# A two-block transformer kernel: the opening sums eight modulation tiles on TensorE and takes the norm statistics per token

## What is computed

```python
cond = jax.nn.silu(c)                                   # c: (1, 1024)
mod = cond @ w_ada[layer] + b_ada[layer]                # (1, 3072)
shift, scale, gate = jnp.split(mod, 3, axis=-1)
h = rmsnorm(x, g_pre[layer]) * (1.0 + scale[:, None, :]) + shift[:, None, :]
z = h @ w_in                                            # first projection of the even mixer
```

## Time and profile before

| | before |
|---|---|
| median of 3 runs | 2442.03 us (2441.51 to 2445.28) |
| profiled execution, its time | 2443.99 us |
| profiled execution, its span | 2442.2 us |
| busy: PE, PEld, DVE, ACT, POOL | 2232.5, 1718.2, 1502.3, 931.8, 13.1 us |
| DMA | 228.51 MB, mean 94 GB/s over the span, about 410 GB/s from 12 to 45 us |

### The profile page before, as it was taken

The page is one execution under the profiler, slowest core; times in us unless marked ns, Lnnn a source line. Parts: engine busy times, 40 slices in busy tenths (PEclk is TensorE's granted clock), DMA queues, the critical chain, the costliest instruction groups (busy, mean ns, idle before and its releaser), DMA issues.

```text
span 2442.2 us, 26914 instructions
## 1 busy us (share of the span) xinstructions
PE 2232.5 (91%) x10142; PEld 1718.2 (70%) x10142; DVE 1502.3 (62%) x2722; ACT 931.8 (38%) x1712; POOL 13.1 (1%) x15
## 2 busy tenths in 40 slices
PE   4898999999899999988999999888888859999998
PEld 2665567776665776667788887777777647888886
DVE  6566675666345479966565564777777764433333
ACT  3233544344232343333233234555555543332331
POOL 1000000000000000000000000000000000000000
PEclk8998998999898889988999999999999978999998
DMA  7422211332212311123555552111111102222321
GB/s 286 155 104 69 68 65 61 121 121 104 87 52 70 138 44 52 35 79 121 197 190 181 181 181 70 44 44 44 44 44 44 44 0 69 99 92 95 103 92 55
DMA packets 65984, 228.51 MB, mean 94 GB/s; under 512 B 7104, under 2 KB 9280, under 8 KB 65728
## 3 DMA queue, kind: packets, MB, share of 16 engines
q1 hardware_dynamic: 65856, 226.79, 26.5%
HBM read 224.67 MB, written 2.10 MB: 93 GB/s over the span
## 4 chain that ended last, share of the span: by engine, by line
PE 67%; DVE 19%; ACT 7%; issue 4%; DMA 3%; SPq 0%; DVEq 0%; ACTq 0%
PE bank L376 17%; PE bank L377 16%; PE bank L378 16%; DVE arena L1529 5%; PE bank L1008 3%; PE bank L1033 3%; DMA w_raw<-weights_dram 2%; PE bank L678 2%; DVE arena L1759 2%; PE bank L1676 2%; DVE w_lo L314 1%; DVE arena L1791 1%; PE bank L1021 1%; DVE arena L1792 1%; PE bank L1010 1%
## 5 line engine op out<-in xcount | busy, mean ns | idle before, releaser
L376 PE MATMUL bank<-h_hi,w_hi 128*128 128x512 f32 (+1 forms) x1616 | 669.9, 415 | 60.7 <-DVE h_lo L645 20.4
L378 PE MATMUL bank<-h_hi,w_lo 128*128 128x512 f32 (+1 forms) x1616 | 642.4, 398 | 0.0
L377 PE MATMUL bank<-h_lo,w_hi 128*128 128x512 f32 (+1 forms) x1616 | 642.4, 398 | 0.0
L314 DVE TENSOR_TENSOR w_lo<-w_raw,w_hi 128x1024 fp32r<-128x1024 f32 (+3 forms) x290 | 333.5, 1150 | 191.2 <-ACT w_hi L305 190.2
L305 ACT ACTIVATE w_hi<-w_raw 128x1024 fp32r<-128x1024 f32 (+3 forms) x293 | 292.3, 998 | 415.5 <-DMA w_raw<-weights_dram 241.3
L376 PEld LDWEIGHTS bank<-h_hi,w_hi 128*128 128x128 f32 (+1 forms) x1616 | 310.9, 192 | 143.7 <-issue 68.8
L378 PEld LDWEIGHTS bank<-h_hi,w_lo 128*128 128x128 f32 (+1 forms) x1616 | 310.2, 192 | 69.4
L377 PEld LDWEIGHTS bank<-h_lo,w_hi 128*128 128x128 f32 (+1 forms) x1616 | 311.6, 193 | 63.4 <-issue 4.1
L376 PE MATMUL bank<-a_hi_t,w_hi 128*128 128x512 f32 x512 | 203.3, 397 | 1.9 <-DVE a_lo_t L1457 1.9
L377 PE MATMUL bank<-a_lo_t,w_hi 128*128 128x512 f32 x512 | 203.2, 397 | 0.0
L378 PE MATMUL bank<-a_hi_t,w_lo 128*128 128x512 f32 x512 | 203.0, 397 | 0.0
(11 more groups left out here) (237 smaller groups left out, 2596.8 us busy)
## 6 DMA issues: line engine op xcount, KB each, us to landing
w_raw<-weights_dram SPq DMA_DIRECT2D x261, 512.0 KB, 4.1
ada_raw<-ada_dram SPq DMA_DIRECT2D x128, 512.0 KB, 3.6
arena<-ada_dram SPq DMA_DIRECT2D x8, 1024.0 KB, 16.6
w_raw<-weights_dram SPq DMA_DIRECT2D x16, 256.0 KB, 2.8
xT<-x_dram SPq DMA_DIRECT2D x1, 2048.0 KB, 10.1
out_dram<-xT SPq DMA_DIRECT2D x8, 256.0 KB, 2.7
tables<-tables_dram SPq DMA_DIRECT2D x1, 1280.0 KB, 19.2
w_raw<-weights_dram SPq DMA_DIRECT2D x8, 144.0 KB, 3.5
```

The source lines that it names most:

```text
L314: eng.tensor_tensor(WL[:, slot, 0:w], RAW[:, raw, 0:w], WH[:, slot, 0:w].bitcast(F32), ALU.subtract).then_inc(lower_half(n)[0], 1)
L376: nc.tensor.matmul(o, WH[:, slot, cols], self.hi(k), start=(k == 0), stop=False)
L377: nc.tensor.matmul(o, WH[:, slot, cols], self.lo(k), start=False, stop=False)
L378: last = nc.tensor.matmul(o, WL[:, slot, cols], self.hi(k), start=False, stop=(k == self.K - 1))
```

## The change

The scale tile of each chunk is summed by PE instead of DVE: the tile is stored in the layout of weights, and eight fp32 products of one column each (128x128 weights, one column of the activated condition) accumulate into one PSUM column (`pe_part`). DVE then makes the gain from that PSUM column with one instruction (1 + b_ada is prepared once), and the bias of the shift goes in as the starting value of its sum. The products for chunk 0 stand in the list at place 0, those for chunk k + 1 stand in the projection ahead of chunk k's nine products (`ahead`). The first norm becomes a `TokenNorm`. Its scaling steps get places 0.55, 1.55, ... and `first_hi`/`first_lo` keep place 1.6, so that ACT's splitting of the first three weight tiles now comes behind the `h_hi` of chunks 0 and 1. On SP the vectors and the two tables are issued ahead of `xT`. The core of the diff:

```diff
+    put("cond", chunked(I["c"][0]))
...
+    for k in range(C):
+        out[2 * k + 1] = tile_of(I["w_ada"][0], 128 * (C + k))
...
                 for k in range(self.K):
+                    if self.ahead:
+                        self.ahead(pe, k)
                     for t in range(self.outer):
                         if k == 0:
                             pe.wait_ge(*lower_half(self.n0 + t))
...
+            def __init__(self, numbers):
+                self.steps, self.numbers = 2 * C, numbers
+                self.scaled = signal("first_scales").take(C)
+                self.plus_one = signal("mod_ready").take(1)
+                for b in numbers:
+                    bank_read[b] = (ada_summed, 2 * C)
+
+            def pe_part(self, pe, k):
+                if k == 0:
+                    pe.wait_ge(cond_ready.sem, cond_ready.at(2))
+                pe.wait_ge(first_ada[k], 16)
+                if k >= 2:
+                    pe.wait_ge(ada_summed, 2 * k - 2)
+                for j in range(C):
+                    last = nc.tensor.matmul(bank[self.numbers[k % 2]][:, k:k + 1], first_tiles[:, 2 * k + 1, j * P:(j + 1) * P], vec("cond", j),
+                                            start=(k < 2 and j == 0), stop=True, skip_group_check=True)
+                last.then_inc(self.scaled.sem, 1)
+
+            def pe_step(self, pe, k):
+                if k == 0:
+                    self.pe_part(pe, 0)
+
+            def ahead(self, pe, k):
+                if k + 1 < C:
+                    self.pe_part(pe, k + 1)
+
+            def dve_step(self, dve, i):
+                k = i // 2
+                if i % 2:
+                    self.gain(dve, k)
+                    return
                 if k == 0:
                     dve.wait_ge(cond_ready.sem, cond_ready.at(1))
                     dve.wait_ge(vectors_in, 16)
+                    nc.vector.tensor_scalar(GAIN[:, 8:16], vec("b_ada0", C, C), 1.0, None, ALU.add).then_inc(self.plus_one.sem, 1)
+                    dve.wait_ge(self.plus_one.sem, self.plus_one.at(1))
                 dve.wait_ge(first_ada[k], 16)
-                for part in range(2):
...
-                dve.wait_ge(ada_summed, 2 * k + 2)
-                nc.vector.tensor_tensor(MOD[:, k:C + k + 1:C], MODRAW[:, k:C + k + 1:C], vec("b_ada0", k, C + 1)[:, ::C], ALU.add).then_inc(self.read.sem, 1)
-                dve.wait_ge(self.read.sem, self.read.at(k + 1))
-                nc.vector.tensor_scalar(GAIN[:, k:k + 1], MOD[:, C + k:C + k + 1], 1.0, vec("g_pre", k), ALU.add, ALU.mult).then_inc(self.gained.sem, 1)
+                nc.vector.tensor_tensor_reduce(first_tiles[:, 2 * k, :], first_tiles[:, 2 * k, :], COND[:], 1.0, vec("b_ada0", k), ALU.mult, ALU.add,
+                                               MOD[:, k:k + 1]).then_inc(ada_summed, 1)
+
+            def gain(self, dve, k):
+                dve.wait_ge(self.scaled.sem, self.scaled.at(k + 1))
+                nc.vector.tensor_scalar(GAIN[:, k:k + 1], bank[self.numbers[k % 2]][:, k:k + 1], GAIN[:, 8 + k:9 + k], vec("g_pre", k), ALU.add, ALU.mult).then_inc(ada_summed, 1)
                 dve.wait_ge(ada_summed, 2 * k + 2)
...
             act.wait_ge(cond_in_sbuf, 16)
             nc.scalar.activation(COND[:], COND[:], ACT.Silu).then_inc(cond_ready.sem, 1)
+            act.wait_ge(vectors_in, 16)
+            nc.scalar.activation(vec("cond", 0, 8), vec("cond", 0, 8), ACT.Silu).then_inc(cond_ready.sem, 1)
...
-            n1 = Norm(XT, C, lambda k: GAIN[:, k:k + 1], lambda k: MOD[:, k:k + 1], HH, HL, 0,
-                      scratch=(view(72, (2, S)), view(76, (2, S)), None, view(80, (S,)), None), ready=[(x_here, 16), (ones_here, 16)])
-            weave((n1, -1, 0.1, 0, C), (FirstAda(), 0, 1), (n1, 1.5, 1, C, C + 1), (Do(act=first_hi, pool=first_lo), 1.6, 1), (n1, 2.6, 0.75, C + 1, 2 * C + 2))
+            n1 = TokenNorm(XT, C, lambda k: GAIN[:, k:k + 1], [after(x_here, 15)] * C, hi=HH, lo=HL, bias=lambda k: MOD[:, k:k + 1], scratch_kb=72)
+            first = FirstAda((5, 6))
+            weave((Do(pe=lambda pe: pe.wait_ge(ones_here.sem, 16), act=lambda act: act.wait_ge(vectors_in, 16)), -2, 1), (n1, -1, 0.1, 0, C), (n1, 0.2, 1, C, C + 1),
+                  (first, 0, 0.5), (n1, 0.55, 1, C + 1, 2 * C + 1), (Do(act=first_hi, pool=first_lo), 1.6, 1), (n1, 7.6, 1, 2 * C + 1, 2 * C + 2))
...
-            a1 = Project(12, C, P, HH, HL, [], plain_evac(Z, 0), chunks=n1.split, ada=ada_next(range(12)), outer=3)
+            a1 = Project(12, C, P, HH, HL, [], plain_evac(Z, 0), chunks=n1.split, ada=ada_next(range(12)), outer=3, ahead=first.ahead)
...
             sp.dma_start(COND[:], cond_in[:, 0, :]).then_inc(cond_in_sbuf, 16)
-            sp.dma_start(XT[:], x_in.rearrange("(c p) s -> p c s", p=P)).then_inc(x_here.sem, 16)
             sp.dma_start(VEC[:], vec_in).then_inc(vectors_in, 16)
             sp.dma_start(TAB[:, 0:2 * P], tab_in[:, 0:2 * P]).then_inc(ones_here.sem, 16)
+            sp.dma_start(XT[:], x_in.rearrange("(c p) s -> p c s", p=P)).then_inc(x_here.sem, 16)
```

More of the change, by code:

```diff
@@ L51 @@
     ("lam", 256), ("subln", 1), ("norm1", 16), ("norm2", 16), ("dw_w", TAPS * 8), ("dw_b", 8),
-    ("ln_g", 8), ("ln_b", 8), ("lb", 16), ("gn", 8), ("final", 8), ("eps", 1), ("zero", 1)])
+    ("ln_g", 8), ("ln_b", 8), ("lb", 16), ("gn", 8), ("final", 8), ("eps", 1), ("zero", 1), ("cond", 8)])
 TABLES, NTAB = columns([("ident", P), ("ones", P), ("perm64", P), ("perm96", P), ("causal", P),
@@ L351, in build, with __init__ @@
         class Project(Stage):
-            def __init__(self, count, K, M, hi, lo, ready, evac, evac_engine="act", dve_work=None, chunks=None, ada=None, banks=(0, 1, 2, 3), parts=1, outer=1):
-                self.ada, self.parts, self.outer = ada or {}, parts, outer
+            def __init__(self, count, K, M, hi, lo, ready, evac, evac_engine="act", dve_work=None, chunks=None, ada=None, banks=(0, 1, 2, 3), parts=1, outer=1, ahead=None):
+                self.ada, self.parts, self.outer, self.ahead = ada or {}, parts, outer, ahead
                 self.steps = count * parts + (1 if parts > 1 else 0) - (outer - 1)
@@ L493, in dve_step @@
                     dve.wait_ge(vectors_in, 16)
+                    nc.vector.tensor_scalar(GAIN[:, 8:16], vec("b_ada0", C, C), 1.0, None, ALU.add).then_inc(self.plus_one.sem, 1)
+                    dve.wait_ge(self.plus_one.sem, self.plus_one.at(1))
                 dve.wait_ge(first_ada[k], 16)
-                for part in range(2):
-                    t, to = 2 * k + part, C * part + k
-                    nc.vector.tensor_tensor_reduce(first_tiles[:, t, :], first_tiles[:, t, :], COND[:], 1.0, 0.0, ALU.mult, ALU.add,
-                                                   MODRAW[:, to:to + 1]).then_inc(ada_summed, 1)
+                nc.vector.tensor_tensor_reduce(first_tiles[:, 2 * k, :], first_tiles[:, 2 * k, :], COND[:], 1.0, vec("b_ada0", k), ALU.mult, ALU.add,
[3 more added lines that the diff above has]
+                nc.vector.tensor_scalar(GAIN[:, k:k + 1], bank[self.numbers[k % 2]][:, k:k + 1], GAIN[:, 8 + k:9 + k], vec("g_pre", k), ALU.add, ALU.mult).then_inc(ada_summed, 1)
                 dve.wait_ge(ada_summed, 2 * k + 2)
-                nc.vector.tensor_tensor(MOD[:, k:C + k + 1:C], MODRAW[:, k:C + k + 1:C], vec("b_ada0", k, C + 1)[:, ::C], ALU.add).then_inc(self.read.sem, 1)
-                dve.wait_ge(self.read.sem, self.read.at(k + 1))
-                nc.vector.tensor_scalar(GAIN[:, k:k + 1], MOD[:, C + k:C + k + 1], 1.0, vec("g_pre", k), ALU.add, ALU.mult).then_inc(self.gained.sem, 1)
-                dve.wait_ge(self.gained.sem, self.gained.at(k + 1))
         first_tiles = view(0, (ADA_FIRST, D))
@@ L512, in ada_tile @@
             if a == 48:
-                dve.wait_ge(cond_ready.sem, cond_ready.at(2))
+                dve.wait_ge(cond_ready.sem, cond_ready.at(3))
             dve.wait_ge(ada_arrived[slot], 16 * (place // ADA_RING + 1))
@@ L660, in __init__ @@
                 self.sq, self.t, self.h = view(scratch_kb, (2, S)), view(scratch_kb + 4, (2, S)), view(scratch_kb + 8, (2, S))
-                self.total = view(scratch_kb + 12, (S,))
+                self.total = view(scratch_kb + 12, (S,)) if added else None
                 self.steps = 2 * n + 2
@@ L830, in dve @@
                 if self._dve: self._dve(e)
-        cond_ready = signal("cond_ready").take(2)
+        cond_ready = signal("cond_ready").take(3)
         consts_ready = signal("consts_ready").take(4)
```

## The result

The changed kernel takes **2465.09 us** (median of 4 runs, 2460.48 to 2468.74), the kernel before 2443.66 us (4 runs, 2441.51 to 2446.87): ratio **1.0086**, 95% interval 1.0064 to 1.0107. It is 21.4 us slower. The profiled execution of the changed kernel took 2468.74 us, its span is 2467.0 us, 24.8 us over that of before.

A forecast was written before the change was run, and what follows sets the result against it. PE holds 67% of the chain, DVE sets the pace from 46 to 62 us. Low clock throughout gives +41.5 us, clock rises reduce it to +36; 2442.0 + 36 = 2478 us, range 2460 to 2486.

The forecast's parts named there:

- the mechanism of the opening: Chunk loop: PE's one-column products, three DVE instructions and PE's nine products run one after the other, in six cycles.
- statistics' products over: Opening on PE: 32 one-column products for the sums of squares, 13.8 us at the low clock, end at 27.2 us.
- POOL's third weight tile: Weight-tile splitting, now behind chunk 1's `h_hi`: POOL done at 46.0 us, where before it was near 33 us.
- a cycle at the low clock: One chunk of the projection: 3.4 + 2.0 + 3.85 = 9.3 us, against 4.18 before.
- sets at the high clock within the loop: Chunk loop: three clock rises worth 1.6 us each, which with 0.7 us of dense work lower +41.5 to +36 us.
- first output tile emptied: ACT empties the first output tile behind the eight chunks: near 99 us, against 63.09 before.
- from there to PE's resumption: Chain behind the first output tile: PE resumes 14.1 us after that tile is complete, as before.
- the rival with the high clock: Opening: clock high throughout or for most cycles, shift +10 to +20 us, 2452 to 2466 us; chance 0.2.
- Faster: Chunk loop: chunk k+1's products don't hold up chunk k's nine; DVE's 2.9 us is the cycle, -8 us, 2434; chance 0.02.
- one-column work neither raises nor keeps the clock: PE in the opening: one-column products leave the clock low, so PE is counted low until the projection.
- Absorbed: PE's resumption hangs on DVE, not the first output tile: up to 7 us vanish, +29, 2471; within the forecast's 0.55.
- I carry the shift of that one moment to the end at full size: From PE's resumption (77.11 us before) to the end: the opening's shift, +36 us, reaches the end undiminished.

The follow-up runs named there:

- experiment 9: Changed kernel plus eight more unused columns in the vectors, buffers behind them 64 bytes further than before the change: 2476.93 us, ratio 1.0138 to the kernel before.
- experiment 2: Changed kernel with the one-column products of chunk k + 2, not k + 1, ahead of chunk k's nine products: 2446.59 us (one run).
- experiment 3: Changed kernel with all eight sets of one-column products ahead of the projection and the weight tiles split at place 0.3: 2446.73 us (one run).
- experiment 1: Changed kernel with the splitting of the first three weight tiles moved from place 1.6 to 0.3: 2464.32 us (one run).
- experiment 6: The kernel before, unchanged, profiled once more: 2441.36 us.
- experiment 10: Statistics as before the change, sums of chunks 0 to 2 early on DVE, only scale tiles 3, 4, 5 on PE before the projection: 2433.02 us, ratio 0.9952.
- experiment 11: Kernel before with only the sums of chunks 0, 1 and 2 put ahead of the norm's reciprocal in DVE's list: 2445.95 us, ratio 1.0007.
- 12: Kernel before with the 32-byte gap ahead of the arena and the sums of chunks 0 to 2 ahead of the reciprocal: 2431.60 us, ratio 0.9950.
- experiment 7: Kernel before with eight unused columns added to the vectors and nothing else: 2434.65 us against 2443.21, ratio 0.9963.
- 8: Kernel before with a 32-byte gap directly ahead of the arena, so the arena alone moves: 2431.25 us against 2442.16, ratio 0.9953.

## Why the prediction was right, and where it was not

The sign and the mechanism of the opening held, and the range holds the measured time. The size did not: the forecast was 2478 us, 36 more than before, and the runs show 2465.09, 21.4 more. Step by step, forecast against the profile of the changed kernel:

| step | forecast | measured |
|---|---|---|
| statistics' products over | 27.2 us | 26.97 |
| spreading over | 32.8 | 32.3 |
| `h_hi` of chunk 1 | 38.0 | 37.35 |
| POOL's third weight tile | 46.0 | 45.35 |
| chunk 0's products over | 47.4 | 46.85 |
| a cycle at the low clock | 9.3 | 9.23 |
| sets at the high clock within the loop | three | two of six |
| first output tile emptied | near 99 | 99.24 |
| from there to PE's resumption | 14.1 | 14.05 |
| end | +36 | +21.4 (median), +24.8 (profiled) |

**What was luck.** The range reached down to 2460 us to take in a higher clock in the opening. The opening was not faster than forecast; the 11 us that brought the time down came from the layout, which the range did not foresee. By the time alone the result would even lie in the range of the rival with the high clock (2452 to 2466), and only the timeline tells them apart. The hit at the mark, 99.24 us for "near 99", is partly luck too: with the layout of experiment 9 the same opening had four sets of six at the high clock and reached it at 95.99.

**Which rivals fell.** Faster: the nine products do wait for the next chunk's set; experiment 2 shows what that order costs, 25 us. High clock throughout: no, but here my view was too coarse. I had argued that one-column work neither raises nor keeps the clock. The first half stands (experiment 3). The second is wrong as a general statement: in experiment 2 the clock stayed up while one-column sets of 1.84 us and dense groups of 2.05 us alternated without a pause. In the changed kernel it fell twice (behind the sets at 74.42 and 81.63 us) where a wait of 1.82 us came on top. The row that I had taken for the fall during fully busy one-column work has such a wait ahead of it, too, 1.38 us. Waits alone did not lower it in the kernel before: from 46 to 62 us the row shows 1.00, though PE waits 1.83 us ahead of 53.81 and 1.85 us ahead of 57.99. So the order was worth more than twice what the waits add up to (six times 1.82 us). That it takes both, one-column work and a wait, is read from these rows; no run varies the wait alone. Absorbed: in all fourteen profiles PE resumes 13.8 to 14.2 us behind the mark, with DVE early or late.

**What each half costs.** By the mark: statistics alone +4.3 us (with the weight tiles early), scale tiles with the late weight tiles +28.5 us; the late weight tiles are some 5 us of it (experiment 1). The two halves don't add up to 36 exactly, because each also moves where the clock rises.

**The step that failed** is "I carry the shift of that one moment to the end at full size". It assumes that everything behind 113 us runs as before. It doesn't: the eight `cond` columns add 32 bytes per partition to the vectors, every buffer behind them moves, and with the arena on a multiple of 64 bytes the products that stream from it run 0.2267 us apart instead of 0.232 and 0.235. I had listed these eight columns as data of the change and not as an edit with a price. The sum is 36.1 (mark) - 11 (distances) = 25.1, against 24.8 measured in the profile; and with the place restored 32.9 against 32.8.

Two sums that close within 0.3 us say more than the profiles can. Take the stretch from PE's resumption to the end and subtract the slow distances: over the fourteen profiles it is 2341.5 to 2353.6 us long. It is shorter where the trace records less time at half clock in it (248 us in experiment 6, with 2344.0 us) and longer where it records more (281 us in experiment 10, with 2353.6 us). So a gain or loss in the opening reaches the end only within about 6 us. Experiments 10 to 12, whose marks are 3 to 7 us earlier than those of their counterparts and whose times are at most 1.6 us shorter, lie within that.

**The price of a one-column product.** At the high clock the sixteen records of a set took 1.84 us, 0.115 each; at the low clock 3.41 us, 0.213 each. PEld was busy nearly throughout (13.73 of the 13.79 us of the statistics), so I read this as the price of the weight loads; no run separates a load from the column behind it. The estimate of 0.107 us worked out from the Trainium skill (TensorE: Matmul & The Clock Gate, section LDWEIGHTS), which names no clock, is near the first. The second is twice that: the price goes with the clock here, and the measurement decides.

## What to carry to other kernels

Work moved to an engine that looks idle goes into that engine's list at a place: ask what stands behind it there, and whether another engine's list closes a loop through it; here the same 64 products, with the token statistics, lengthened the opening by 36 us in one order and by 11 in another (experiment 2), and 24 of them, in PE's idle time, did no harm (experiment 10: its mark is 3.8 us earlier than that of experiment 11, which has none). One column of output doesn't make an fp32 product cheap: it cost 0.23 us at 2.4 GHz and 0.43 us at 1.2 GHz, as much as a dense fp32r product of 512 columns. And try multiples of 64 bytes for the start of buffers that TensorE streams from. When a change adds even a few bytes of SBUF, compare it with a kernel before of the same layout, or the layout is booked as an effect of the change.

## What the runs showed of the hardware that I had not expected

**Where a moving operand starts within 64 bytes changed the pace of its products.** (The moving operand is the one whose 512 columns stream through the weights.) By the kernel's own allocation the arena of the kernel before starts at byte 141,920 of a partition, 32 over a multiple of 64, and `h_hi` at 32,896, a multiple of 64. Products with `h_hi` have a median of 389 ns in every kernel; those with `a_hi_t` and `fox_hi` in the arena have 396 at this start and 64 bytes on, 389 at 32 bytes on. That is 3% of the distance between two products, and 9 to 12 us of the whole (2443.21 to 2434.65 in experiment 7, 2442.16 to 2431.25 in 8, 2465.09 to 2476.93 in 9), about half of what the change lost. Three starts were tried, which are two places within 64 bytes, 0 and 32; all of these products are fp32r with 512 columns at the high clock. Other places were not tried, nor was the stationary operand, which lay on a multiple of 64 in these products throughout. The Trainium skill (SBUF — State Buffer, section Operand start alignment) says which addresses are legal and that its measurements timed nothing; these runs put a time on it.

**The column of the granted clock can say 1.00 while PE runs at half.** Up to the first change that the profiler records the page shows 1.00, in the changed kernel until 77 us. The distances between products tell it: nine products 0.43 us apart from 52 to 56 us. In experiment 2 the column shows 1.00 for the whole opening, so there, too, the rise at 55.6 us is read from the distances.
